# Two attention layers ahead of two mixture-of-experts layers: the output projection as seven block products, with the weight sums re-ordered on GpSimd

## What is computed

```python
for i in range(DEPTH):                                  # DEPTH = 2
    h = rms_norm(x, norm_g[i])
    proj = h @ w_in[i]                                  # 1024 -> 4096, 8 pieces of 512
    rq, rk, rv, rz, mq, mk, mv, mz = jnp.split(proj, cuts, axis=-1)
    r_out = silu(rz) * retention(rotary(rq), rotary(rk), rv, ret_norm_g[i])
    m_out = silu(mz) * moba(rms_norm(mq), rms_norm(mk), mv, rel_bias)
    y = concatenate([r_out, m_out]) @ w_out[i]          # 256 x 1024 times 1024 x 1024
    x = x + y
    gate = sigmoid(rms_norm(x) @ w_ple_gate[i])         # 1024 x 1024
    e = rms_norm(p[i] @ w_ple[i], ple_norm_g[i])        # 256 -> 1024
    x = x + gate * e
```

## Time and profile before

| what | value |
|---|---|
| median of 3 runs | 1579.29 us |
| the profiled execution: its own time | 1580.07 us |
| its span (first to last instruction) | 1578.2 us |
| PE busy / POOL busy, share of the span | 84% / 11% |
| mean granted clock of PE | 0.953 |
| first layers, from the start to PE's last matmul | 0 to 391.5 us |
| output projection, layer 0 / layer 1 | starts at 132.12 / 317.06 us |
| DMA | 498.20 MB, mean 316 GB/s |

### The profile page before, as it was taken

One profiled execution on the slowest core, in us unless ns is written; L12 is line 12 of the kernel. 1 busy time (PEld: TensorE's weight loads), 2 busy tenths in 40 slices (PEclk: granted clock), 3 DMA queues, 4 the chain that ended last, 5 costly groups with the idle time before them and its releaser, 6 DMA issues. The chain is left out here.

```text
span 1578.2 us, 22176 instructions
## 1 busy us (share of the span) xinstructions
PE 1331.1 (84%) x9378; PEld 717.3 (45%) x9378; DVE 424.9 (27%) x838; ACT 278.7 (18%) x544; POOL 180.0 (11%) x122
## 2 busy tenths in 40 slices
PE   9999999999999999776766677899999776666676
PEld 4855456545879564322322323655554232232232
DVE  2543343523565531120000100267321010010011
ACT  2132310323412121210000000114212011011010
POOL 0450033300000005692000000000000000000000
PEclk9999999999999999998898999999999889899799
DMA  9923542254641499999999999954799999999997
GB/s 382 344 82 132 187 160 107 80 187 161 231 159 32 165 358 425 429 427 429 428 429 428 429 427 430 385 189 166 285 385 428 425 428 428 427 427 428 426 427 325
DMA packets 44867, 498.20 MB, mean 316 GB/s; under 512 B 6656, under 2 KB 8960, under 8 KB 12544
## 3 DMA queue, kind: packets, MB, share of 16 engines
q1 hardware_dynamic: 44800, 497.22, 76.8%
HBM read 495.11 MB, written 2.10 MB: 315 GB/s over the span
## 5 line engine op out<-in xcount | busy, mean ns | idle before, releaser
L2839 PE MATMUL banks<-weight_ring,arena 128*32 128x512 f32 x1472 | 212.4, 710 | 130.0 <-DMA weight_ring<-in_moe_weights 129.9
L2767 DVE TENSOR_TENSOR arena<-arena,banks 64x512 f32<-64x512 f32 x32 | 22.1, 690 | 666.6 <-ACT arena L2712 666.6
L2839 PEld LDWEIGHTS banks<-weight_ring,arena 128*32 128x32 f32 x1472 | 45.6, 119 | 284.0 <-issue 142.1
L2824 PE MATMUL banks<-arena,x 128*128 128x64 f32 x1024 | 119.7, 276 | 0.0
L2824 PEld LDWEIGHTS banks<-arena,x 128*128 128x128 f32 x1024 | 119.0, 195 | 0.1
L323 PE MATMUL banks<-weight_ring,hT 128*128 128x512 f32 x256 | 112.3, 593 | 0.0
L2712 ACT ACTIVATE arena<-banks 64x512 f32<-64x512 f32 x32 | 18.9, 590 | 501.0 <-PE banks L2839 501.0
L2850 PE MATMUL banks<-weight_ring,arena 128*32 128x512 f32 x728 | 86.0, 596 | 22.4 <-DMA weight_ring<-in_moe_weights 10.4
L2880 PE MATMUL banks<-arena 64*128 64x512 f32 x240 | 59.6, 615 | 21.0 <-ACT arena L2718 21.0
L323 PEld LDWEIGHTS banks<-weight_ring,hT 128*128 128x128 f32 x256 | 48.1, 190 | 57.2 <-issue 56.9
L2839 PE MATMUL banks<-arena 128*32 128x512 f32 x352 | 58.2, 688 | 16.9 <-DMA arena<-in_moe_weights 16.9
(11 more groups left out here) (526 smaller groups left out, 1744.3 us busy)
## 6 DMA issues: line engine op xcount, KB each, us to landing
weight_ring<-in_moe_weights SPq DMA_DIRECT2D x137, 2048.0 KB, 26.9
weight_ring<-in_ring_weights SPq DMA_DIRECT2D x35, 2048.0 KB, 9.4
arena<-in_moe_weights SPq DMA_DIRECT2D x18, 2048.0 KB, 44.5
spare_weights<-in_moe_weights SPq DMA_DIRECT2D x10, 2048.0 KB, 43.9
mix<-in_moe_weights SPq DMA_DIRECT2D x9, 2048.0 KB, 48.1
arena<-in_moe_weights SPq DMA_DIRECT2D x17, 1024.0 KB, 42.1
x_normed<-in_moe_weights SPq DMA_DIRECT2D x9, 1024.0 KB, 39.1
hT<-in_moe_weights SPq DMA_DIRECT2D x9, 1024.0 KB, 47.5
```

The costliest lines, as they stand in the source:

```text
L2767: dve.tensor_tensor(hid[0:2 * CAP, :], sil[0:2 * CAP, :], b_gu[2 * CAP:4 * CAP, :], ALU.mult).then_inc(s_h, 1)
L2824: ins = pe.matmul((b_x, b_dn)[k // 4][:, k % 4 * 2 * CAP:(k % 4 + 1) * 2 * CAP], g.x[:, tt, k * P:(k + 1) * P], Pr[:, tt, :], start=(tt == ...
L2839: ins = pe.matmul(b_gu[q:q + CAP, :], xg[:, 2 * quarter + k, e * CAP:(e + 1) * CAP], up_w(where, quarter, e)[:, which, k, :], start=(quart ...
```

## The change

`w_out` goes the way of the two pairs. Seven block products O1, O2, O6, O5, O3, O7, O4 (`out_product`) take the place of the four quarters; their input sums SO1 to SO4 are made by POOL of `mixT`, and their weight sums of chunks 8 and 9. DVE adds each product from PSUM straight to the quarters of x that it belongs to (`x_sum`, 14 additions for 4). The third weight sum of all pairs is written over `wx[:, 0:4]`, after P1 (or O1) has read it, and no longer into `spare`; the two halves of `spare` hold T2 in turn. POOL's order is new, and so is ACT's: e_out goes in between the squares. Chunk 8 is now free at y(7), the last block product, and chunk 9 at y(5). The gate products use banks 5, 0, 4, 1.

```diff
-    T2, T3 = (g.spare[:, i * 2048:(i + 1) * 2048].rearrange("p (k n) -> p k n", n=HALF) for i in range(2))
+    T2s = [g.spare[:, i * 2048:(i + 1) * 2048].rearrange("p (k n) -> p k n", n=HALF) for i in range(2)]
+    T2 = lambda l, which: T2s[(3 * l + which) % 2]
...
-                                  q.y(3), q.y(4), q.e(4), q.g(3), q.g(4))):
+                                  q.y(7), q.y(5), q.e(4), q.g(3), q.g(4))):
...
+    GATE_BANK = (5, 0, 4, 1)
+    O1, O2, O6, O5, O3, O7, O4 = range(1, 8)
+    OUT = 2
+    MX11, MX12, MX21, MX22 = (g.mixT[:, 4 * k:4 * k + 4, t * P:(t + 1) * P] for t in range(2) for k in range(2))
+    SO1, SO2, SO3, SO4 = (rqk_flat[:, i * 512:(i + 1) * 512].rearrange("p (k t) -> p k t", k=HT) for i in range(4))
+    X11, X12, X21, X22 = (g.x[:, tt, ch * HALF:(ch + 1) * HALF] for tt in range(2) for ch in range(2))
...
-                for tt in range(TT):
-                    for ch in range(2):
-                        act.wait_ge(*q.x(2 * tt + ch + 1))
-                        n.squares(act, tt, ch)
-                    n.root(act, tt)
+                act.wait_ge(*q.x(1))
+                n.squares(act, 0, 0)
                 e_out(q, 0)
+                act.wait_ge(*q.x(2))
+                n.squares(act, 0, 1)
+                n.root(act, 0)
+                act.wait_ge(*q.x(3))
+                n.squares(act, 1, 1, 0)
                 e_out(q, 1)
+                act.wait_ge(*q.x(4))
+                n.squares(act, 1, 0, 1)
+                n.root(act, 1)
...
-                add_out(q, 0)
+                dve.wait_ge(*q.y(O1))
+                x_sum(q, X12, 0).then_inc(q.u.sem, 1)
+                x_sum(q, X21, 0).then_inc(q.u.sem, 1)
+                x_sum(q, X22, 0).then_inc(q.u.sem, 1)
+                x_sum(q, X11, 0).then_inc(q.u.sem, 1)
+                dve.wait_ge(*q.y(O2))
+                x_sum(q, X11, 1, 4).then_inc(q.x.sem, 1)
+                dve.wait_ge(*q.y(O6))
...
+                dve.wait_ge(*q.y(O5))
+                x_sum(q, X12, 5, 5).then_inc(q.u.sem, 1)
+                x_sum(q, X22, 5, 6).then_inc(q.u.sem, 1)
                 n.eps(dve, 0)
-                add_out(q, 1)
+                dve.wait_ge(*q.y(O3))
+                x_sum(q, X12, 0, 8).then_inc(q.x.sem, 1)
                 n.scale(dve, 0)
-                add_out(q, 2)
+                dve.wait_ge(*q.y(O7))
+                x_sum(q, X22, 1, 9).then_inc(q.x.sem, 1)
+                x_sum(q, X21, 1, 7).then_inc(q.u.sem, 1)
...
             for l in range(DEPTH):
                 q = layer[l]
-                for pair in range(2):
...
+                was = layer[l - 1] if l else None
+                sum1(l, 0)
+                sum2(l, 0, *([done(was, 1, P6), was.t4(2)] if l else []))
+                pool.wait_ge(*q.qkt(4))
+                inputs(q, 0, (S1, S2, S3, S4), (A11, A12, A21, A22))
+                sum1(l, 1)
+                sum2(l, 1, *([was.y(O6), was.t4(3)] if l else []))
+                sum3(l, 0, done(q, 0, P1))
+                sum1(l, OUT)
+                sum4(l, 0, done(q, 0, P2))
+                sum2(l, OUT, done(q, 0, P6), q.t4(1))
+                sum3(l, 1, done(q, 1, P1))
+                sum4(l, 1, done(q, 1, P2))
+                pool.wait_ge(*q.mT(4))
+                inputs(q, 4, (SO1, SO2, SO3, SO4), (MX11, MX12, MX21, MX22))
+                sum3(l, OUT, q.y(O1))
+                sum4(l, OUT, q.y(O2))
...
                 pe.wait_ge(*q.mT(2))
-                natural(l, 8, g.mixT, 0, 0, q.y.sem)
+                out_product(l, O1)
                 mix_transposes(q, 1)
-                natural(l, 9, g.mixT, 1, 1, q.y.sem)
-                pe.wait_ge(*q.mT(4))
-                pe.wait_ge(*formed(q, 1, C21))
-                natural(l, 8, g.mixT, 2, 4, q.y.sem)
-                n.transposes(pe, 0)
-                natural(l, 9, g.mixT, 3, 5, q.y.sem)
+                out_product(l, O2)
                 pe.wait_ge(s_tok[l], 16)
                 e_in(l, 0)
+                for n_ in (O6, O5, O3, O7):
+                    out_product(l, n_)
                 e_in(l, 1)
+                n.transposes(pe, 0)
+                out_product(l, O4)
                 n.ready(pe, 0)
```

More of the change, by code:

```diff
@@ L745, in combine, with x_sum @@
                 TT_(out, in0, bank, ALU.subtract if n == C21 else ALU.add).then_inc(q.cd.sem, 1)
-            def add_out(q, j):
-                dve.wait_ge(*q.y(j + 1))
-                TT_(g.x[part(j)], g.x[part(j)], ps[OUT_BANK[j]], ALU.add).then_inc(q.x.sem, 1)
+            def x_sum(q, dst, bank, was=None, op=ALU.add):
+                if was is not None:
+                    dve.wait_ge(*q.u(was))
+                return TT_(dst, dst, ps[bank], op)
             def e_eps(q, tt):
@@ L879, in _, with weights, sum1, sum2 @@
         def _(pool):
+            sub = lambda out, left, right: pool.tensor_tensor(out, left, right, ALU.subtract)
+            def weights(l, which):
+                return (g.chunk(pool, per * l + c) for c in (PAIR_CHUNKS + ((8, 9),))[which])
+            def sum1(l, which):
+                wx, wy = weights(l, which)
+                sub(wy[:, 0:4], wy[:, 0:4], wx[:, 0:4]).then_inc(layer[l].ts.sem, 1)
+            def sum2(l, which, *read):
+                wx, wy = weights(l, which)
+                pool.wait_ge(*layer[l].ts(2 * which + 1))
+                for when in read:
+                    pool.wait_ge(*when)
+                sub(T2(l, which), wy[:, 4:8], wy[:, 0:4]).then_inc(layer[l].ts.sem, 1)
@@ new lines, in sum3, with sum4 @@
+            def sum3(l, which, p1):
+                wx, wy = weights(l, which)
+                pool.wait_ge(*layer[l].ts(2 * which + 2))
+                pool.wait_ge(*p1)
+                sub(wx[:, 0:4], T2(l, which), wx[:, 0:4]).then_inc(layer[l].t3.sem, 1)
+            def sum4(l, which, p2):
+                wx, wy = weights(l, which)
+                pool.wait_ge(*layer[l].ts(2 * which + 2))
+                pool.wait_ge(*p2)
+                sub(wx[:, 4:8], T2(l, which), wx[:, 4:8]).then_inc(layer[l].t4.sem, 1)
@@ L880, in _, with inputs @@
+            def inputs(q, base, out, left):
+                (s1, s2, s3, s4), (a11, a12, a21, a22) = out, left
+                pool.tensor_tensor(s1, a21, a22, ALU.add).then_inc(q.as_.sem, 1)
+                pool.wait_ge(*q.as_(base + 1))
+                sub(s2, s1, a11).then_inc(q.as_.sem, 1)
+                pool.wait_ge(*q.as_(base + 2))
+                sub(s4, a12, s2).then_inc(q.as_.sem, 1)
+                sub(s3, a11, a21).then_inc(q.as_.sem, 1)
             for l in range(DEPTH):
                 q = layer[l]
-                for pair in range(2):
[L883 to L902, removed]
@@ L925, in product @@
                 wx, wy = (g.chunk(pe, per * l + c) for c in PAIR_CHUNKS[pair])
[L926 to L929, removed]
+                left, right = {P1: (A11, wx[:, 0:4]), P6: (S2, T2(l, pair)), P2: (A12, wx[:, 4:8]), P5: (S1, wy[:, 0:4]),
+                               P3: (S4, wy[:, 4:8]), P7: (S3, wx[:, 0:4]), P4: (A22, wx[:, 4:8])}[n]
+                if n in (P5, P6):
+                    pe.wait_ge(*q.ts(2 * pair + {P5: 1, P6: 2}[n]))
+                if n == P7:
+                    pe.wait_ge(*q.t3(pair + 1))
+                if n == P4:
+                    pe.wait_ge(*q.t4(pair + 1))
                 if n in (P5, P6, P3, P7):
@@ L943, in product, with out_product @@
                 ins.then_inc(q.prj.sem, 1)
+            def out_product(l, n):
+                q = layer[l]
+                wx, wy = (g.chunk(pe, per * l + c) for c in (8, 9))
+                left, right, bank = {O1: (MX11, wx[:, 0:4], 0), O2: (MX12, wx[:, 4:8], 1), O6: (SO2, T2(l, OUT), 4),
+                                     O5: (SO1, wy[:, 0:4], 5), O3: (SO4, wy[:, 4:8], 0), O7: (SO3, wx[:, 0:4], 1),
+                                     O4: (MX22, wx[:, 4:8], 4)}[n]
+                if n in (O5, O6):
+                    pe.wait_ge(*q.ts(2 * OUT + {O5: 1, O6: 2}[n]))
+                if n in (O5, O6, O3, O7):
+                    pe.wait_ge(*q.as_(4 + {O5: 1, O6: 2, O3: 3, O7: 4}[n]))
+                if n in (O6, O5):
+                    pe.wait_ge(*formed(q, 1, {O6: C21, O5: C22}[n]))
+                if n == O7:
+                    pe.wait_ge(*q.t3(OUT + 1))
+                    pe.wait_ge(*q.x(1))
+                if n == O4:
+                    pe.wait_ge(*q.t4(OUT + 1))
+                if n in (O3, O4):
+                    pe.wait_ge(*q.u({O3: 4, O4: 7}[n]))
+                for k in range(HT):
+                    ins = pe.matmul(ps[bank], left[:, k, :], right[:, k, :], start=(k == 0), stop=(k == HT - 1))
+                ins.then_inc(q.y.sem, 1)
             def mix_transposes(q, tt):
```

33 lines of the change are left out of this document (18 added, 15 removed).

## The result

The changed kernel takes **1585.18 us** (median of 7 runs, 1581.37 to 1588.08), beside it the kernel before 1579.40 (7 runs, 1578.73 to 1581.40). The ratio is 1.0032, interval 1.0022 to 1.0042: 5.8 us slower. I had forecast 1575.4 and a range of 1572.6 to 1578.4, so size and direction are wrong.

What follows compares the result with a forecast made beforehand. PE's back-to-back instructions were taken to bound the first layers: 6.86 us saved, less 0.1 and 2.85 of waits, gives 3.9 us less, 1575.4 us from a median of 1579.29; range 1572.6 to 1578.4.

Steps and rivals of the forecast that it cites:

- What PE saves, 6.86 us: First layers' output projection: 56 matmul records per layer instead of 64, 3.43 us a layer, 6.86 us for two.
- No wait in the new output projection: Products and transposes there find their inputs ready, apart from 0.05 us a layer at the transposes.
- POOL against DVE's addition: Layer 0: POOL's first sum of pair 1 delays DVE's fourth rotary addition; PE waits 2.85 us before the scores.
- Rival 1: PE's clock falls behind the new wait before the scores, costing at most 1.66 us: 1577.0 us; chance 0.34.
- rival 2: DVE's addition gets ahead of POOL's sum and the fourth product hardly waits: 1572.4 to 1574.5 us; chance 0.08.
- I expect them to start earlier and otherwise run as before: Expert slices after the first layers' barrier: a microsecond saved or lost by PE before it is one at the end.
- Rival 4: DVE's addition misses POOL's gap twice, PE waits 12 us behind pair 1's first product: 1586 us; chance 0.05.
- The barrier to the end as long as before: Sign for the profile after: the time from the barrier ending the first layers to the kernel's end stays unchanged.

Runs made afterwards that it cites:

- e8: e4's kernel with 4 tiny matmuls (16 instructions) added at PE's start; 1571.46 us, ratio 0.9948 to the kernel before.
- e1: The changed kernel once more, unchanged, for a second profile and more runs; 1584.9 us, ratio 1.0037 to the kernel before.
- e2: The changed kernel with 20 instead of 22 filler matmuls at the end of the first layers; 1585.96 us, ratio 1.0035 to the kernel before.
- e5: The changed kernel with 8 tiny matmuls (32 instructions) added at PE's start; 1576.19 us, ratio 0.9983 to the kernel before.
- e4: The changed kernel with POOL's order altered: pair 0's third weight sum before pair 1's first, its fourth before pair 1's second; 1580.98 us, ratio 1.0009.
- e9: e4's kernel with the odd layer's 2 MB spare_weights load issued later, behind the small matmuls it ran beside; 1575.45 us, ratio 0.9975 to the kernel before.
- e10: e4's kernel with four tiny matmuls (16 instructions) at the start of the odd layer; 1574.75 us, ratio 0.9973 to the kernel before.

## Why the prediction was wrong, point by point

**What PE saves, 6.86 us: right.** The projection takes 29.30 and 29.22 us where it took 32.65. The cleanest view is e8, whose P1 starts at 69.44 us as before's does, without a wait behind it: its even layer starts at 385.93 us for 392.71, 6.8 us earlier. At the end it is 1579.54 - 1571.46 = 8.1 us, the 6.86 and 1.2 us that the working does not account for.

**No wait in the new output projection: right.** The transposes come 0.03 us late, and O6, O4 and the normed transposes wait for nothing, in both layers.

**POOL against DVE's addition: right in kind, too definite in size.** POOL's sum started at 70.34 (forecast 70.6), and in layer 1 the addition took 0.69 us without a wait, as forecast. I gave 2.85 us, and 1.21, 3.35 and 3.84 were seen, or 2.48 at P4 instead. POOL's sum started at 70.34, 71.18, 70.60 and 71.38 us in after, e1, e2 and e5, and P1 at 70.65, 69.34, 68.26 and 68.66; where POOL was first, an earlier P1 meant a longer wait behind it. I took both from one execution. In e2 POOL was 0.10 us ahead of the addition, in e5 the addition 0.29 ahead of POOL. Rival 1 occurred in e2 and rival 2 in e5, whose first layers differ from the changed kernel's by idle matmuls alone; they are outcomes of a race that can fall differently in each execution, and I had put them down as separate worlds. With the wait moved away e4 is 3.9 us faster than e1.

**"I expect them to start earlier and otherwise run as before, so a microsecond saved or lost by PE in the first layers is one at the end": this step failed.** The stages behind do start earlier, but the odd layer doesn't run as before, since its instructions lie elsewhere in the blocks in which they are fetched. Against before, e1's profile has the even layer 3.3 us earlier; then the burst costs 4.7 us more and the stretch behind it 2.1. The even layer's stage is 0.5 us longer, and the stretch from its experts to the odd layer 1.4 (444.03 for 442.65 us). That last stretch was 442.65 to 443.27 us in six of the profiles and 444.0 to 444.4 in six, with one of the changed kernel in each set, so it is a matter of the execution and not of the change. What goes with it is the clock: in e1, e2, e4, e9 and e10 the granted clock falls to 0.50 for 3.4 us from 34 us behind the start of the experts (a product in e1 takes 1.06 us there for 0.59 in after), and the next group of products starts 1.7 us later than in the others; in e8 it falls at 66 us. In the six shorter ones it does not fall in the first 70 us. Why it falls there in some executions stays open. Sum: 5.4 us slower in the profile, 5.3 in the medians.

**Rival 4, slower at 1586**, met the time by another road and is no success: the addition never missed POOL's first gap. "The barrier to the end as long as before" was the sign named in advance, and it was the one that failed.

The row that could have warned me stood in the trace of before: a gap of 0.31 us for "issue" within 192 small matmuls at 452.07. The Trainium skill, "Runtime: NRT & Kernel Launch", section "Instruction fetch mechanics", says that the sequencer fetches blocks of 16 KB, 256 instructions, through a DMA queue of its own, and that crossing a block is mostly hidden. The trace agrees on the 16 KB (0.85 MB in 52 packets), does not show how many instructions a packet holds, and differs on the cost here: a wait of 1.44 to 1.78 us, and 5.3 to 6.9 us with the clock.

What stays open: when PE asks for a block is not in the trace, only when it comes. Why a packet came in the midst of the same load at 20.4 us, but one for a cut seven records further on only at 24.5 or later, I can't say. The load was moved only in the kernel with the new order of POOL, not in the changed kernel as it was, and but for the changed kernel each variant was profiled once.

## What to carry to other kernels

Where an engine runs many short instructions in a row, its instruction fetch is a resource like any other: look for gaps that end on "issue" inside such a burst, and count what a change adds or removes ahead of it. If an edit that saved time in its own stage loses it in code that it doesn't touch, shift the program by some 16 instructions, or move the load beside the burst, before judging the edit. And take a term that hangs on the race of a landing with another engine from several executions, as a spread.

## What the runs showed of the hardware that I had not expected

- 128 small matmuls in the code (256 records, 28.8 ns each) outran the fetch of their own instructions when the DMA engines were full, and four tiny matmuls ahead of them, at either of two places, mended that.
- The clock fell to 1.2 GHz behind a gap of only 1.44 to 1.78 us between small matmuls, and stayed there for 6.8 to 10.2 us. Behind 3.35 us between large products in e1 it did not fall, and behind 3.84 in e2 it fell for 3.4 us. In the even layer gaps of up to 1.55 us left the small matmuls behind them at their pitch (43 records in 0.91 us behind gaps of 0.98 to 1.55 us in five profiles). So the length of the gap alone does not tell.
- A load on another queue held back a 16 KB packet of instructions by about 2.8 us (24.7 us in e4, 21.9 in e9, both from the start of the odd layer).
